# Inverse of the delta rule's unit triangular matrices: from full 128x128 tiles to compact 64x64 diagonal blocks

## The chip, the core and the metric

The kernel runs on one core of one Trainium2 chip. The metric is the device time of one execution in microseconds (us); the time before is the median of three executions. The engines are TensorE (PE in the profile, its weight loads PEld), VectorE (DVE), ScalarE (ACT), GpSimd (POOL) and SyncE (SP, which issues most transfers).

## What is computed

The program is one inference step of a two-layer encoder trunk, for a prompt of 512 rows and a second group of 32 rows. Its first mixer holds a gated delta rule with 4 heads, computed in chunks. For every chunk of L rows and every head the reference builds a unit lower triangular matrix and solves with it:

```python
gam = jnp.cumsum(g, axis=-1)
dec = jnp.exp(jnp.where(incl, gam[..., :, None] - gam[..., None, :], -jnp.inf))
kk = jnp.einsum('bhid,bhjd->bhij', k, k)
a_mat = jnp.eye(L) + jnp.where(strict, beta[..., :, None] * kk * dec, 0.0)
sol = lax.linalg.triangular_solve(a_mat, rhs, left_side=True, lower=True)
```

The kernel works on tiles of 128 rows. It inverts the matrix explicitly and keeps the transposed inverse in `a.xt`; the next phase multiplies with it. The rest of the program (projections, the other head group, attention, two mixtures of experts) is not touched.

## The kernel before

The program is a list of phases. Each phase is one or more blocks in which every engine has an instruction stream of its own; a barrier of all engines ends a block. The change lies in the second block of `phase_gdn_inverse`. Ahead of that block, the first block leaves the decayed products of the keys in `lm` (128 partitions, 5 tiles, 4 heads, 128 columns). Behind it comes `phase_gdn`, whose first work on the engines waits for the barrier.

The inverse is found by doubling. `LEV` is 7; at level l the blocks of 2^l rows on the diagonal are already inverted, and pairs of them are joined. A step is one level of one row tile t (all 4 heads together), and there are 7 x 5 = 35 steps, levels outside and tiles inside. One step i goes through four engines:

- POOL masks `lm` with the level's mask into `ll` (L1254, 128x512 elements).
- PE computes `ptt` from `ll` and `xt` (L1267, 4 matmuls of 128x128, one per head); the source calls this `product_t(i)`.
- ACT copies `ptt` to `tt` (L1294).
- PE computes `pp` (L1278, not at the last level) and `ppt` (L1279), 8 matmuls, called `correction(i)`; DVE subtracts them from `x` (L1303) and from `a.xt` (L1304).

PE's stream is product_t(i), then correction(i - 1). All buffers between the engines are double, and semaphores (`ll_ready`, `tt_done`, `tt_ready`, `p_done`, `x_ready`) count steps. The identity of level 0 is read from the constants `cst`.

One earlier phase, `phase_gla`, is quoted in the prediction because it already runs 64x64 matmuls (L1047, L1049, L1052). A 64x64 matmul uses one quarter of the array: the half of the input partitions is the row half, the half of the output partitions is the column half. Its output `gla_ps` is a PSUM tensor with 2 KB of each partition for each head, and `rows(h)` picks the row half by the head:

```python
for l in range(LEV - 1):
    for c, h in ((0, hs[0]), (1, hs[1]), (1, hs[0]), (0, hs[1])):
        m = em[rows(h), t % 2, l, at_col(c)]
        nc.tensor.matmul(ps[blk(c), h, l, :], m, m, start=True, stop=True)
...
for h in hs:
    last = nc.tensor.matmul(ps[0:HB, h, LEV, :], em[rows(h), t % 2, LEV - 1, at_col(0)],
```

Of the kernel before, what the change touches and what calls it, by code (L numbers as in the profile page):

```python
# [53 lines left out]
K_CS = K_ML + LEV * P  # L54
# [10 lines left out]
def constants():  # L65
# [7 lines left out]
    for l in range(LEV):  # L73
        m = 1 << l
        blk = i // m
        c[:, K_ML + l * P:K_ML + (l + 1) * P] = (blk[:, None] == blk[None, :] + 1) & (blk[None, :] % 2 == 0)
# [1111 lines left out]
def phase_gdn_inverse(g, a):  # L1188
# [5 lines left out]
    with ExitStack() as ctx:  # L1194
# [3 lines left out]
        x = sb("x", [P, NT, NH, P])  # L1198
        ll = sb("ll", [P, 2, NH, P])
        tt = sb("tt", [P, 2, NH, P])  # L1200
# [42 lines left out]
        ll_ready, tt_done, tt_ready, p_done, x_ready = map(sem, ("ll_ready", "tt_done", "tt_ready", "p_done", "x_ready"))  # L1243
        steps = LEV * NT
        ident = g.c(K_ID, P)
        with nc.Block() as block:
            @block.gpsimd
            def _(pool):
                for i in range(steps):
                    l, t = divmod(i, NT)  # L1250
                    if i >= 2:
                        pool.wait_ge(tt_done, i - 1)
                    mask = g.c(K_ML + l * P, P).unsqueeze(1).to_broadcast([P, NH, P])
                    nc.gpsimd.tensor_tensor(ll[:, i % 2], lm[:, t], mask, ALU.mult).then_inc(ll_ready, 1)  # L1254

            @block.tensor
            def _(pe):
                def product_t(i):

                    l, t = divmod(i, NT)  # L1260
                    pe.wait_ge(ll_ready, i + 1)
                    if l:
                        pe.wait_ge(x_ready, i - NT + 1)
                    if i >= 2:
                        pe.wait_ge(tt_ready, i - 1)
                    for h in range(NH):
                        last = nc.tensor.matmul(ptt[:, i % 2, h, :], ll[:, i % 2, h, :], a.xt[:, t, h, :] if l else ident, start=True, stop=True)  # L1267
                    last.then_inc(tt_done, 1)

                def correction(i):  # L1270

                    l, t = divmod(i, NT)
# [9 lines left out]
                for i in range(steps):  # L1282
                    product_t(i)
                    if i:
                        correction(i - 1)
                correction(steps - 1)

            @block.scalar
            def _(act):
                for i in range(steps):  # L1290
# [3 lines left out]
                    nc.scalar.copy(tt[:, i % 2], ptt[:, i % 2]).then_inc(tt_ready, 1)  # L1294

            @block.vector
            def _(dve):
                eye = ident.unsqueeze(1).to_broadcast([P, NH, P])
                for i in range(steps):
                    l, t = divmod(i, NT)  # L1300
                    dve.wait_ge(p_done, i + 1)
                    if l < LEV - 1:
                        nc.vector.tensor_tensor(x[:, t], x[:, t] if l else eye, pp[:, i % 2], ALU.subtract)  # L1303
                    nc.vector.tensor_tensor(a.xt[:, t], a.xt[:, t] if l else eye, ppt[:, i % 2], ALU.subtract).then_inc(x_ready, 1)  # L1304
# [1388 lines left out]
```

## Time and profile before

| | |
|---|---|
| median of three executions | 2523.39 us |
| lowest and highest | 2520.73 and 2523.8 us |
| the profiled execution | 2520.12 us |
| its span in the profile | 2518.2 us |
| mean granted TensorE clock | 0.907 of 2.4 GHz |
| PE busy over the span | 2066.4 us (82%) |
| DVE, ACT, POOL busy | 1600.8, 1301.5 and 261.8 us |

Times of the profile are counted from the start of the span. The span is 1.9 us shorter than the execution's own time, and the profiled execution lies 3.3 us below the median. Matmuls are recorded with modelled ends, so consecutive records overlap; the distance from start to start is the pace. An fp32 matmul leaves two records. The granted clock is 1.00 at 2.4 GHz and 0.50 at 1.2 GHz.

### The profile page before, as it was taken

The page shows a single profiled execution, that of the slowest core. Times are in us where ns is not written, and L with a number is a line of the kernel's source. Part 1 is how long each engine was busy: PE and PEld are TensorE (multiplying, and loading weights), DVE is VectorE, ACT ScalarE, POOL GpSimd, SP SyncE. Part 2 cuts the span into 40 slices and gives each one's busy share as a digit, 9 for nine tenths or more (in the row PEclk, how much of TensorE's full clock was granted, in tenths as well). Part 3 has the DMA queues.
Part 4 walks back from the last instruction along what each step waited for, and adds up shares of the span by engine and source line. Part 5 has one row for each costly group of instructions (what it writes and reads, how often), then busy time and mean ns, then how long its engine had stood idle before and what let it go on. Part 6 is the DMA issues. An engine that isn't in the chain of part 4 may idle for free. (4 is left out here: it accounts for less than half of the span.)

```text
span 2518.2 us, 32513 instructions
## 1 busy us (share of the span) xinstructions
PE 2066.4 (82%) x12936; PEld 1700.9 (68%) x12936; DVE 1600.8 (64%) x1729; ACT 1301.5 (52%) x1514; POOL 261.8 (10%) x329
## 2 busy tenths in 40 slices
PE   2689777886574999999998188998759999999990
PEld 1679774886574888888887054555747888888870
DVE  0345107454646888888886513665368888888883
ACT  1233612222323777777775342443237777777763
POOL 0123120330000010101110010000000010101000
PEclk6789888997786999999999598999969999999995
DMA  9167450000343899999997512002338999999974
GB/s 335 51 247 284 171 195 10 3 5 1 132 143 127 321 367 372 374 380 380 366 364 263 200 69 105 1 1 79 121 116 318 372 367 365 366 366 370 369 272 169
DMA packets 160041, 561.47 MB, mean 223 GB/s; under 512 B 33757, under 2 KB 39930, under 8 KB 126738
## 3 DMA queue, kind: packets, MB, share of 16 engines
q1 hardware_dynamic: 137938, 539.04, 57.9%
q0 software_dynamic: 21952, 20.32, 2.4%
q8 instruction: 106, 1.74, 0.3%
q14 instruction: 45, 0.37, 0.0%
HBM read 557.84 MB, written 50.70 MB: 242 GB/s over the span
## 5 line engine op out<-in xcount | busy, mean ns | idle before, releaser
L1954 DVE TENSOR_TENSOR ex_wl<-ring,ex_wh 128x2048 fp32r<-128x2048 f32 x384 | 867.9, 2289 | 112.5 <-ACT ex_wh L1909 112.5
L1909 ACT CAST ex_wh<-ring 128x2048 fp32r<-128x2048 f32 x384 | 712.4, 1910 | 0.0
L238 PE MATMUL ex_p<-ex_wh,ex_xh 128*128 128x512 f32 x1024 | 414.3, 405 | 8.3 <-DVE ex_xl L1959 8.3
L238 PE MATMUL ex_p<-ex_wl,ex_xh 128*128 128x512 f32 x1024 | 402.3, 393 | 0.0
L238 PE MATMUL ex_p<-ex_wh,ex_xl 128*128 128x512 f32 x1024 | 401.7, 392 | 0.0
L238 PEld LDWEIGHTS ex_p<-ex_wh,ex_xh 128*128 128x128 f32 x1024 | 194.5, 190 | 46.1 <-DVE ex_xl L1959 9.9
L238 PEld LDWEIGHTS ex_p<-ex_wl,ex_xh 128*128 128x128 f32 x1024 | 194.0, 189 | 42.7
L238 PEld LDWEIGHTS ex_p<-ex_wh,ex_xl 128*128 128x128 f32 x1024 | 194.5, 190 | 36.7
L238 PE MATMUL ex_py<-ex_wh,ex_gh 128*128 128x512 f32 x512 | 200.2, 391 | 2.8 <-DVE ex_gl L1975 2.8
L238 PE MATMUL ex_py<-ex_wl,ex_gh 128*128 128x512 f32 x512 | 200.2, 391 | 0.0
L238 PE MATMUL ex_py<-ex_wh,ex_gl 128*128 128x512 f32 x512 | 199.9, 390 | 0.0
L1823 POOL DMA_INDIRECT yrow<-ex_y,put x64 | 64.7, 1010 | 1026.9 <-ACT ex_y L1944 1026.9
L1922 ACT CAST ex_gh<-ex_pg 128x512 fp32r<-128x512 f32 x64 | 37.6, 588 | 155.1 <-PE ex_pg L1862 155.1
L1944 ACT COPY ex_y<-ex_py 128x1024 f32<-128x1024 f32 x64 | 65.1, 1017 | 92.4 <-PE ex_py L238 92.4
L238 PEld LDWEIGHTS ex_py<-ex_wh,ex_gh 128*128 128x128 f32 x512 | 96.6, 189 | 23.4 <-DVE ex_gl L1975 3.3
L238 PEld LDWEIGHTS ex_py<-ex_wh,ex_gl 128*128 128x128 f32 x512 | 96.6, 189 | 20.1
L238 PEld LDWEIGHTS ex_py<-ex_wl,ex_gh 128*128 128x128 f32 x512 | 96.5, 189 | 20.1
L1959 DVE TENSOR_TENSOR ex_xl<-ex_px,ex_xh 128x1024 fp32r<-128x1024 f32 x64 | 78.4, 1224 | 33.3 <-ACT ex_xh L1916 33.3
L270 DVE TENSOR_TENSOR ab_wl<-ring,ab_wh 128x2048 fp32r<-128x2048 f32 (+1 forms) x15 | 32.3, 2160 | 89.1 <-ACT ab_wh L265 89.1
L238 PE MATMUL ab_z<-ab_hh,ab_wh 128*128 128x288 f32 (+3 forms) x272 | 79.9, 294 | 4.4 <-DVE ab_wl L270 4.4
L1847 PEld LDWEIGHTS ex_px<-cst,ex_x 128*128 128x128 f32 x512 | 67.7, 190 | 22.2 <-DMA ex_x<-hrow,take 17.2
L1847 PE MATMUL ex_px<-cst,ex_x 128*128 128x128 f32 x512 | 68.7, 278 | 16.9 <-DMA ex_x<-hrow,take 16.9
(414 smaller groups left out, 3811.3 us busy)
## 6 DMA issues: line engine op xcount, KB each, us to landing
ring<-in_moe_w SPq DMA_DIRECT2D x384, 1024.0 KB, 7.3
ring<-in_ada_w SPq DMA_DIRECT2D x24, 2048.0 KB, 12.2
ring<-in_ab_w_in SPq DMA_DIRECT2D x7, 2048.0 KB, 9.7
mod<-mod SPq DMA_DIRECT2D x16, 512.0 KB, 7.1
cb_y<-yrow SPq DMA_DIRECT2D x16, 512.0 KB, 9.6
xres<-x SPq DMA_DIRECT2D x12, 512.0 KB, 2.7
x<-xres SPq DMA_DIRECT2D x12, 512.0 KB, 9.4
ring<-in_ab_w_out SPq DMA_DIRECT2D x2, 2048.0 KB, 11.9
```

What stands on the lines that cost most here:

```text
L238: ins = nc.tensor.matmul(out, a, b, start=first and n + m == 0, stop=last and n == len(terms) - 1 and m == 2)
L270: self.g.nc.vector.tensor_tensor(l, w, h.bitcast(F32), ALU.subtract).then_inc(self.lo_ready, 1)
L1823: pool.indirect_dma_start(out=io["yrow"], out_offset=bass.IndirectOffsetOnAxis(ap=rt.put[:, e:e + 1], axis=0), in_=y[:, e % 2, :], in_offs ...
L1847: last = nc.tensor.transpose(px[:, k, :], x[:, e % 2, k:D:KT], g.c(K_ID, P))
L1909: nc.scalar.copy(part(wh, u), g.view(base + u)).then_inc(hi_ready, 1)
L1922: nc.scalar.copy(gh[:], pg[:]).then_inc(gh_ready, 1)
L1944: nc.scalar.copy(y[:, (e - 1) % 2, :].rearrange("p (a n) -> p a n", a=2), py[:]).then_inc(y_ready, 1)
L1954: nc.vector.tensor_tensor(part(wl, u), g.view(base + u), part(wh, u).bitcast(F32), ALU.subtract).then_inc(lo_ready, 1)
L1959: nc.vector.tensor_tensor(xl[:, e % 2], px[:], xh[:, e % 2].bitcast(F32), ALU.subtract).then_inc(xl_ready, 1)
```

## The change

The 128x128 matrix of a tile is seen as two 64x64 diagonal blocks and one 64x64 block below them. The first six levels touch only the diagonal blocks. They are now held compactly: rows 0 to 63 of a tensor hold the upper block, rows 64 to 127 the lower one, both in 64 columns, so that every tensor of a step has 256 columns for the 4 heads. Each matmul of 128x128 becomes two of 64x64, one for each block, in different quarters of the array. Level 0 has no correction, since the blocks of one row are their own inverses: only `ptt` is computed, and DVE forms `x` and `xt` with four operations on 64 partitions. The last level computes only the block below the diagonal. For tile 4, which has 32 rows, levels 5 and 6 are dropped, which leaves 33 steps. POOL first sets the whole of `a.xt` to zero, and ACT first copies the diagonal blocks to `lmc`. The level masks in the constants shrink from 7 x 128 to 6 x 64 columns.

```diff
-K_CS = K_ML + LEV * P
+K_CS = K_ML + (LEV - 1) * HB
...
+        lmc = sb("lmc", [P, NT, NH, HB])
+        x, xt = sb("x", [P, NT, NH, HB]), sb("xt", [P, NT, NH, HB])
...
-        steps = LEV * NT
+        steps = [(l, t) for l in range(LEV) for t in range(NT) if t < NT - 1 or 1 << l < DSEQ]
+        place = {step: i for i, step in enumerate(steps)}
+        blocks = [slice(HB * c, HB * c + HB) for c in range(2)]
...
+                nc.gpsimd.memset(a.xt[:], 0.0).then_inc(zero_set, 1)
+                for i, (l, t) in enumerate(steps):
+                    if l == LEV - 1:
+                        break
+                    if l == 0:
+                        pool.wait_ge(lc_ready, t + 1)
                     if i >= 2:
                         pool.wait_ge(tt_done, i - 1)
+                        if steps[i - 2][0] == 0:
+                            pool.wait_ge(x_ready, i - 1)
+                    mask = g.c(K_ML + l * HB, HB).unsqueeze(1).to_broadcast([P, NH, HB])
+                    nc.gpsimd.tensor_tensor(ll[:, i % 2], lmc[:, t], mask, ALU.mult).then_inc(ll_ready, 1)
...
                     for h in range(NH):
-                        last = nc.tensor.matmul(ptt[:, i % 2, h, :], ll[:, i % 2, h, :], a.xt[:, t, h, :] if l else ident, start=True, stop=True)
+                        if l == LEV - 1:
+                            last = nc.tensor.matmul(ptt[blocks[0], i % 2, h, 0:HB], lm[blocks[1], t, h, 0:HB], a.xt[blocks[1], t, h, HB:P],
+                                                    start=True, stop=True)
+                            continue
+                        for r in blocks:
+                            last = nc.tensor.matmul(ptt[r, i % 2, h, 0:HB], ll[r, i % 2, h, :], xt[r, t, h, :] if l else g.cst[r, K_ID + r.start:K_ID + r.stop],
+                                                    start=True, stop=True)
                     last.then_inc(tt_done, 1)
...
                     for h in range(NH):
-                        if l < LEV - 1:
-                            nc.tensor.matmul(pp[:, i % 2, h, :], tt[:, i % 2, h, :], x[:, t, h, :] if l else ident, start=True, stop=True)
-                        last = nc.tensor.matmul(ppt[:, i % 2, h, :], x[:, t, h, :] if l else ident, tt[:, i % 2, h, :], start=True, stop=True)
...
+                        for r in blocks:
+                            nc.tensor.matmul(pp[r, i % 2, h, 0:HB], tt[r, i % 2, h, :], x[r, t, h, :], start=True, stop=True)
+                            last = nc.tensor.matmul(ppt[r, i % 2, h, 0:HB], x[r, t, h, :], tt[r, i % 2, h, :], start=True, stop=True)
...
+                for t in range(NT):
+                    nc.scalar.copy(lmc[blocks[0], t], lm[blocks[0], t, :, 0:HB])
+                    nc.scalar.copy(lmc[blocks[1], t], lm[blocks[1], t, :, HB:P]).then_inc(lc_ready, 1)
...
+                    if l == 0:
+                        dve.wait_ge(tt_done, i + 1)
+                        for r in blocks:
+                            nc.vector.tensor_tensor(x[r, t], eye(r), ll[r, i % 2], ALU.subtract)
+                            ins = nc.vector.tensor_tensor(xt[r, t], eye(r), ptt[r, i % 2, :, 0:HB], ALU.subtract)
+                        ins.then_inc(x_ready, 1)
+                        continue
                     dve.wait_ge(p_done, i + 1)
+                    if l == LEV - 1:
+                        nc.vector.tensor_scalar(a.xt[blocks[0], t, :, HB:P], ppt[blocks[0], i % 2, :, 0:HB], -1.0, None, ALU.mult).then_inc(x_ready, 1)
+                        continue
```

Two places of the instruction streams show the change. The first is POOL's stream at the start of the block, where `inv_ll` is the masked matrix; before, it begins with masks of 512 columns.

```order
L1254 ISA
L1254 TENSOR_TENSOR inv_ll<-inv_lm,cst 128x512 x2
L1254 TENSOR_TENSOR inv_ll<-inv_lm,cst 128x512 [waits inv_tt_done] x33
L1246 UNCONDITIONAL_BRANCH
```

Now POOL starts with the zeroing of `a.xt` (named gdn_xt), and its masks have 256 columns.

```order
L1255 MEMSET gdn_xt 128x2560
L1266 ISA
L1266 TENSOR_TENSOR inv_ll<-inv_lmc,cst 128x256 [waits inv_lc_ready] x2
L1266 TENSOR_TENSOR inv_ll<-inv_lmc,cst 128x256 [waits inv_x_ready,inv_tt_done,inv_lc_ready] x3
L1266 TENSOR_TENSOR inv_ll<-inv_lmc,cst 128x256 [waits inv_x_ready,inv_tt_done] x2
L1266 TENSOR_TENSOR inv_ll<-inv_lmc,cst 128x256 [waits inv_tt_done] x22
```

The masks of tiles 2 to 4 at level 0, and of the two steps behind them, now also wait for `x_ready`, since DVE itself reads `ll` at level 0. The second place is PE's stream at the start of the block. Before, eight matmuls of the first two products stand ahead of the first correction.

```order
L1267 MATMUL inv_ptt<-cst,inv_ll 128x128 x8
L1278 MATMUL inv_pp<-cst,inv_tt 128x128
L1279 MATMUL inv_ppt<-inv_tt,cst 128x128
L1278 MATMUL inv_pp<-cst,inv_tt 128x128
L1279 MATMUL inv_ppt<-inv_tt,cst 128x128
```

Now all five products of level 0 and the first two of level 1 stand there, in 56 matmuls of 64x64.

```order
L1285 MATMUL inv_ptt<-cst,inv_ll 64x64 x40
L1285 MATMUL inv_ptt<-inv_xt,inv_ll 64x64 x16
L1304 MATMUL inv_pp<-inv_x,inv_tt 64x64
L1305 MATMUL inv_ppt<-inv_tt,inv_x 64x64
L1304 MATMUL inv_pp<-inv_x,inv_tt 64x64
L1305 MATMUL inv_ppt<-inv_tt,inv_x 64x64
```

What moved: the first correction now belongs to step 5, and in each correction the two matmuls of the upper block stand ahead of the two of the lower block.

## Rows read from the trace of the kernel before

**Rows 1.** Windows of the block: length, busy of PE, PEld, DVE, ACT, POOL; clock, DMA share, GB/s.
```profile
463.20:467.40 4.20, 2.86 (x13) 2.87 (x14) 0.00 (x0) 0.59 (x1) 3.19 (x3) 0.59 0.01 2
467.40:556.30 88.90, 88.13 (x789) 87.94 (x787) 42.00 (x65) 19.89 (x34) 41.23 (x33) 1.00 0.01 1
```
**Rows 2.** Groups by line and shape from 330 to 600 us: busy, mean ns, idle before.
```profile
L1254 POOL TENSOR_TENSOR inv_ll<-inv_lm,cst 128x512 f32<-128x512 f32 x35 | 44.4, 1270 | 143.6 <-SPq L1246 99.8 <-PE inv_ptt L1267 43.8
L1279 PE MATMUL inv_ppt<-inv_tt,inv_x 128*128 128x128 f32 x240 | 43.8, 275 | 0.0
L1278 PE MATMUL inv_pp<-inv_x,inv_tt 128*128 128x128 f32 x200 | 38.7, 275 | 0.0
...
L1294 ACT COPY inv_tt<-inv_ptt 128x512 f32<-128x512 f32 x35 | 20.5, 585 | 72.2 <-PE inv_ptt L1267 72.2
L1304 DVE TENSOR_TENSOR gdn_xt<-gdn_xt,inv_ppt 128x512 f32<-128x512 f32 x30 | 20.4, 682 | 4.0 <-PE inv_ppt L1279 4.0
...
L1303 DVE TENSOR_TENSOR inv_x<-inv_x,inv_pp 128x512 f32<-128x512 f32 x25 | 17.2, 688 | 34.9 <-PE inv_ppt L1279 34.9
```
**Rows 3.** Timeline of the block: its start, one steady step, its end.
```profile
463.23 2.48 POOL L1254 TENSOR_TENSOR inv_ll<-inv_lm,cst 128x512 f32<-128x512 f32 x2 [99.80 <-SPq L1246]
...
464.54 3.40 PE L1267 MATMUL inv_ptt<-cst,inv_ll 128*128 128x128 f32 x16 [5.09 <-POOL inv_ll L1254]
...
472.24 1.06 PE L1267 MATMUL inv_ptt<-cst,inv_ll 128*128 128x128 f32 x8
...
474.92 1.06 PE L1267 MATMUL inv_ptt<-cst,inv_ll 128*128 128x128 f32 x8
...
555.57 0.69 DVE L1304 TENSOR_TENSOR gdn_xt<-gdn_xt,inv_ppt 128x512 f32<-128x512 f32 x1 [0.25 <-PE inv_ppt L1279]
```
**Rows 4.** Timeline of PE in the earlier phase with 64x64 tiles, clock 1.00.
```profile
404.71 0.93 PE L1047 MATMUL gla_ps<-gla_em 64*64 64x64 f32 x48 [1.88 <-DVE gla_qe L1142]
...
405.58 0.27 PE L1047 MATMUL gla_ps<-gla_em 64*64 64x64 f32 x2
405.60 0.28 PE L1052 MATMUL gla_ps<-gla_em 64*64 64x64 f32 x3
405.69 0.82 PE L1047 MATMUL gla_ps<-gla_em 64*64 64x64 f32 x44
...
406.51 0.30 PE L1052 MATMUL gla_ps<-gla_em 64*64 64x64 f32 x4
```
**Rows 5.** The same phase at the lower clock: timeline of PE, and its window.
```profile
435.06 1.56 PE L1047 MATMUL gla_ps<-gla_em 64*64 64x64 f32 x48 [4.84 <-DVE gla_qe L1142]
...
436.77 1.44 PE L1047 MATMUL gla_ps<-gla_em 64*64 64x64 f32 x44
...
433.40:440.10 6.70, 5.04 (x129) 4.60 (x130) 4.57 (x11) 0.19 (x1) 0.00 (x0) 0.50 0.08 22
```
**Rows 6.** Small operations elsewhere: a DVE pair in the timeline, then groups by shape.
```profile
403.81 0.85 DVE L1142 TENSOR_TENSOR gla_qe<-gla_em,gla_qk 64x256 f32<-64x256 f32 x2
...
L1148 DVE TENSOR_TENSOR gla_ket<-gla_ket,gla_ps 128x256 f32<-128x256 f32 x5 | 1.8, 416 | 2.9 <-ACT gla_ket L1105 2.9
L1117 ACT COPY gla_at<-gla_ps 64x256 f32<-64x256 f32 x5 | 1.8, 366 | 24.5 <-DVE gla_mk L1162 24.5
...
L1827 POOL MEMSET ex_x<- 128x2048 f32 x2 | 3.6, 1807 | 590.9 <-POOLq L1666 590.9
```
**Rows 7.** Two stretches with part of the array in use: window and PE's work.
```profile
139.70:143.10 3.40, 3.40 (x9) 2.18 (x9) 1.62 (x3) 1.91 (x3) 1.68 (x3) 0.50 0.11 37
...
139.22 4.76 PE L710 MATMUL ab_z<-w_alpha,lrT 25*128 25x256 f32 x10 [9.49 <-ACT lrT L747]
...
1491.40:1498.20 6.80, 6.80 (x26) 2.58 (x24) 1.59 (x8) 4.04 (x10) 0.00 (x0) 1.00 0.00 0
...
L2255 PE MATMUL mp_p<-ring,mla_hT 128*32 128x384 f32 x14 | 4.7, 486 | 0.0
```
**Rows 8.** The page, GB/s in 40 equal slices of the span.
```profile
GB/s 335 51 247 284 171 195 10 3 5 1 132 143 127 321 367 372 374 380 380 366 364 263 200 69 105 1 1 79 121 116 318 372 367 365 366 366 370 369 272 169
```

More of the change, by code:

```diff
@@ L75, in constants @@
         blk = i // m
-        c[:, K_ML + l * P:K_ML + (l + 1) * P] = (blk[:, None] == blk[None, :] + 1) & (blk[None, :] % 2 == 0)
+        if l < LEV - 1:
+            r, q = i[:, None] % HB >> l, i[None, 0:HB] >> l
+            c[:, K_ML + l * HB:K_ML + (l + 1) * HB] = (r == q + 1) & (q % 2 == 0)
         mid = blk // 2 * 2 * m + m - 1
@@ L1285, in _ @@
                         correction(i - 1)
-                correction(steps - 1)
+                correction(len(steps) - 1)
             @block.scalar
             def _(act):
-                for i in range(steps):
+                for t in range(NT):
+                    nc.scalar.copy(lmc[blocks[0], t], lm[blocks[0], t, :, 0:HB])
+                    nc.scalar.copy(lmc[blocks[1], t], lm[blocks[1], t, :, HB:P]).then_inc(lc_ready, 1)
+                for i, (l, t) in enumerate(steps):
+                    if l == 0:
+                        act.sem_inc(tt_ready, 1)
+                        continue
                     act.wait_ge(tt_done, i + 1)
@@ L1293, in _ @@
                         act.wait_ge(p_done, i - 1)
-                    nc.scalar.copy(tt[:, i % 2], ptt[:, i % 2]).then_inc(tt_ready, 1)
+                    r = blocks[0] if l == LEV - 1 else slice(0, P)
+                    nc.scalar.copy(tt[r, i % 2], ptt[r, i % 2, :, 0:HB]).then_inc(tt_ready, 1)
             @block.vector
             def _(dve):
-                eye = ident.unsqueeze(1).to_broadcast([P, NH, P])
-                for i in range(steps):
-                    l, t = divmod(i, NT)
-                    dve.wait_ge(p_done, i + 1)
-                    if l < LEV - 1:
-                        nc.vector.tensor_tensor(x[:, t], x[:, t] if l else eye, pp[:, i % 2], ALU.subtract)
-                    nc.vector.tensor_tensor(a.xt[:, t], a.xt[:, t] if l else eye, ppt[:, i % 2], ALU.subtract).then_inc(x_ready, 1)
+                ch = g.chain(dve, "dve")
@@ new lines, in _ @@
+                eye = lambda r: g.cst[r, K_ID + r.start:K_ID + r.stop].unsqueeze(1).to_broadcast([HB, NH, HB])
+                dve.wait_ge(zero_set, 1)
+                for i, (l, t) in enumerate(steps):
+                    if l == 0:
+                        dve.wait_ge(tt_done, i + 1)
[3 more added lines that the diff above has]
+                        ins.then_inc(x_ready, 1)
+                        continue
+                    dve.wait_ge(p_done, i + 1)
+                    if l == LEV - 1:
+                        nc.vector.tensor_scalar(a.xt[blocks[0], t, :, HB:P], ppt[blocks[0], i % 2, :, 0:HB], -1.0, None, ALU.mult).then_inc(x_ready, 1)
+                        continue
+                    if t < NT - 1 or 2 << l < DSEQ:
+                        nc.vector.tensor_tensor(x[:, t], x[:, t], pp[:, i % 2, :, 0:HB], ALU.subtract)
+                    if (l + 1, t) in place and l + 1 < LEV - 1:
+                        nc.vector.tensor_tensor(xt[:, t], xt[:, t], ppt[:, i % 2, :, 0:HB], ALU.subtract).then_inc(x_ready, 1)
+                    else:
+                        for r in blocks:
+                            ins = nc.vector.tensor_tensor(a.xt[r, t, :, r], xt[r, t], ppt[r, i % 2, :, 0:HB], ALU.subtract)
+                        ins.then_inc(x_ready, 1)
@@ L1307, in phase_gdn @@
+                g.done(ch, "dve")
 @phase
```

29 lines of the change are left out of this document (15 added, 14 removed).

## The prediction

> **What bounds the block now.** I read the windows first. From 467.40 to 556.30 us PE is busy 88.13 of 88.90 us at a granted clock of 1.00, while DVE has 42.00, POOL 41.23 and ACT 19.89 us of work, and the transfer engines stand at a share of 0.01 [rows 1]. So PE alone bounds the block, and no transfer waits in it. The groups say the same from the other side: PE's two correction groups have no idle time ahead of them, and ACT, DVE and POOL spend theirs waiting for PE [rows 2]. The timeline gives the price of a step: the products of two consecutive steps start at 472.24 and 474.92, 2.68 us apart, for 12 matmuls of 128x128, so 0.223 us each, two records of 0.112 [rows 3]. The block begins at 463.23 with POOL's first mask, and its last work is DVE's subtraction at 555.57, which ends at 556.26 [rows 3]. That is 93.03 us. The barriers at both ends stay, and the next phase starts from the barrier, so whatever the block gains the execution should gain: at 1 to 5 GB/s in the slices around it there is no stream of weights that would have to catch up [rows 8].
>
> **What a 64x64 matmul costs.** The block has none, the earlier phase has. With all four quarters of the array in use, 44 records start within 0.82 - 0.22 = 0.60 us, in 11 rounds of four, so one quarter takes a record each 0.06 us and a matmul of two records 0.12 us [rows 4]. (0.22 is the length of one record, which a last record adds.) The change uses two quarters at a time, upper left and lower right. The nearest row is L1052, two matmuls in two different row halves: its four records fit in 0.30 us [rows 4]. One after the other they would take 3 x 0.06 + 0.22 = 0.40; side by side 0.06 + 0.22 = 0.28. So two halves do run side by side, and a matmul costs 0.06 us in a dense stream of pairs. At 1.2 GHz the same reading gives (1.56 - 0.31) / 11 = 0.11 us for a record [rows 5], so 0.11 us a matmul in pairs and 0.22 alone. The bounds for a step of 24 matmuls at full clock are thus 24 x 0.06 = 1.44 us (pairs) and 24 x 0.12 = 2.88 us (each alone). I take 1.44, because L1052 is nearer.
>
> **Is anything else slower than 1.44 us?** DVE has two subtractions of 128x256, 0.42 us each [rows 6], 0.85 in all; at level 5 the second is split over two halves, and a pair of 64x256 takes 0.85 [rows 6], so 1.27. ACT has 0.37 to 0.38 for a copy of 256 columns, from the 64x256 row [rows 6]. POOL's mask of 512 columns takes 1.27 [rows 2]; half the columns cost between 0.64 and 1.27, and I take 0.68. All stay below 1.44, and the double buffers leave each a whole step, as now, so PE remains the bound through levels 1 to 5.
>
> **The new block, from 463.23.**
> - POOL sets 2560 columns to zero first: 1.81 us for 2048 [rows 6] gives 2.26. It hides nothing and nothing hides it: masks, products and DVE queue behind it. ACT's ten copies to `lmc` lie beside it; the first pair, 0.75 us, is done before the first mask, the rest keep ahead at 0.75 a tile. Uncovered they would cost that 0.75.
> - First mask 0.68, hand-overs 0.15 (in the block before, PE starts 0.07 after POOL's first mask ends [rows 3]), first product of 8 matmuls at the lower clock, 0.88 and 0.2 to finish: DVE starts level 0 at 467.4.
> - Level 0, five steps. DVE needs 4 x 0.425 = 1.70 us for each. But mask i + 2 waits until DVE has finished step i, since DVE reads `ll`, so two steps take 1.70 + 0.68 + 1.1 + 0.3 = 3.8 us, or 1.9 each; 9.5 in all, until 476.9. Step 6's mask waits for the last of them: PE's dense stretch starts at 477.7.
> - Levels 1 to 5, 24 steps (five tiles for levels 1 to 4, four for level 5): 24 x 1.44 = 34.6, less 0.5 for the product of step 5, which is done: until 511.8.
> - Clock. In the window 463.20:467.40 the clock is 0.59, after PE had stood idle, and from 467.40 it is 1.00, 2.9 us after PE's first matmul [rows 1, 3]; in the earlier phase PE works from 435.06 and the clock is still 0.50 up to 440.10 [rows 5]. Level 0 leaves PE idle half of the time, so I let the dense stretch begin at 1.2 GHz and run so for 5 us: 2.5 us lost, until 514.3.
> - Level 6, four steps of four products and four corrections in one quarter each: 0.48 + 0.48, and part of ACT's copy and its hand-overs no longer covered, 1.2 us a step: 4.8, until 519.1.
> - Last record and last DVE operation: 0.8, so 519.9.
>
> The gain is 556.26 - 519.9 = 36.4 us. The constants also shrink by 512 columns, 262 KB; at the first slice's 335 GB/s that is 0.8 us if that load is on the path [rows 8]. I count it as nothing, because the first weights stream beside it, and keep the 0.8 for the range. From the profiled execution's own 2520.12 us the sum gives 2483.7; the median lies 3.3 above that execution, so 2487.
>
> **Rivals.**
> 1. *The pairs overlap less, because of their order.* In a correction the two matmuls of the upper block stand ahead of the two of the lower one. If a matmul could start only after the one written before it, each pair of the same quarter would overlap the next pair in one record only: 2 x (0.24 - 0.06) = 0.36 us for four matmuls, a correction 1.44 and a step 1.92. That is 24 x 0.48 = 11.5 more: 2498.5. Against it: L1047's first two records of the next pair start at 405.58, before the L1052 records at 405.60 that are written ahead of them [rows 4], so a busy quarter doesn't hold up a free one. The Trainium skill (TensorE: Matmul & The Clock Gate, Part 3: Packing small matmuls) says that matmuls start and end in program order, which would bring this rival; the trace just quoted differs, and I go by the trace.
> 2. *The clock stays at 1.2 GHz.* Of the array's 16,384 cells two quarters use half. At 139.22 PE works densely for 4.76 us on 25 rows, and the clock stays 0.50 [rows 7]; against that, 26 records on 32 columns and all rows keep the clock at 1.00 over 6.8 us [rows 7]. The two quarters of a pair cover all rows, so the second row is the nearer one, but it shows only that a high clock stays. A step would cost 24 x 0.11 = 2.64, the levels 1 to 5 take 62.5 instead of 36.6, level 6 2.4 more: the gain shrinks to 8.1, 2515.
> 3. *The two blocks take turns, and it gets slower.* L1052's outputs lie in two separate stretches of 2 KB of PSUM, one for each head. Here the two blocks write the same stretch, `ptt[:, i % 2]`, on different partitions, from different row halves at the same time, and no row shows that. If the array made them take turns, a matmul would cost 0.12 and a step 2.88: 34.6 more, a gain of 1.8, 2521.6, no measurable change. But then only half of the rows would be at work at any time, and the clock would probably stay low as at 139.22: 0.22 a matmul, 5.28 a step, 54 us slower, 2578. It decides from 0.123 us a matmul, where 36.4 us are used up. The Trainium skill (TensorEngine Tiling (Array Packing), Gotcha 1: PSUM Pressure) says that different row tiles can't access one PSUM bank at the same time; no run here shows it yet. By it this rival would hold; without it the sum above.
>
> **Chances.** The forecast 0.60: both of its doubtful rows are near ones. Rival 1 0.12, rival 2 0.14, rival 3 0.12 (0.08 with the low clock, 0.04 without); 0.02 for anything else. The forecast's own range: if the clock rises before the dense stretch (2.5), level 0 runs at 1.70 (1.0), level 6 at 0.96 (1.0) and the constants count (0.8), it is 5.3 lower; with a mask of 0.9 us, a second slow stretch of the clock or level 6 at 1.7 it is about 6 higher: 2481 to 2493. For 8 in 10 the range has to take in rivals 1 and 2: 2480 to 2516, with some 0.14 outside. A measurement of this kernel can tell about 0.2%, 5 us, from no change: faster 0.87, same 0.05, slower 0.08.
>
> **What the profile after would show.** POOL's first instruction is a memset of 2.2 to 2.3 us. Products of consecutive steps in levels 1 to 4 start 1.44 us apart; 1.92 would be rival 1, 2.64 with a clock of 0.50 rival 2, 2.88 or 5.28 rival 3. DVE's groups of four 64x256 operations start 1.9 us apart. The granted clock reaches 1.00 within 5 us of the dense stretch. The block lasts about 57 us from POOL's first work to DVE's last, and the phases behind it are as long as before, but for a few us where the clock rises earlier or later in their gaps. The prediction is wrong if pairs that write one stretch of PSUM don't overlap, if half of the cells don't raise the clock, or if the time gained returns in a later phase.

## The result, and the profile after

| | before | after |
|---|---|---|
| median | 2522.06 us (4 runs) | 2485.39 us (4 runs) |
| lowest and highest | 2519.77 and 2523.8 us | 2483.24 and 2495.84 us |
| profiled execution, its span | 2520.12, 2518.2 us | 2486.33, 2484.5 us |
| block of the inverse, first work to DVE's last | 93.03 us | 55.45 us |

The changed kernel is 1.3% faster: the ratio is 0.9867, with a 95% interval from 0.9853 to 0.9881. The forecast was 2487.0 us, and a block of 56.7 us.

The windows of the new block come first (length, busy of PE, PEld, DVE, ACT, POOL, clock, DMA share, GB/s); they answer to [rows 1].

```profile
464.00:468.30 4.30, 1.21 (x22) 1.22 (x24) 0.00 (x0) 4.03 (x10) 3.63 (x3) 0.67 0.00 0
468.30:479.30 11.00, 5.24 (x80) 4.30 (x77) 8.80 (x20) 0.37 (x1) 3.94 (x6) 0.50 0.00 1
479.30:482.40 3.10, 3.10 (x57) 3.10 (x59) 0.18 (x1) 0.37 (x1) 1.35 (x2) 0.50 0.03 8
482.40:514.00 31.60, 31.16 (x1050) 30.89 (x1049) 17.11 (x46) 8.20 (x22) 14.54 (x20) 1.00 0.02 4
514.00:519.50 5.50, 4.53 (x107) 4.14 (x103) 4.15 (x11) 1.46 (x4) 0.00 (x0) 1.00 0.01 3
```

Read the second row first. In these 11 us of level 0, PE works 5.24 us, and DVE works 8.80: PE is no longer the bound there. In the third row PE is full, but at the clock of 0.50; only from 482.40 on is the block as it was before, PE full at 1.00.

The timeline of the same block (start, length, engine, line) answers to [rows 3].

```profile
464.04 2.23 POOL L1255 MEMSET gdn_xt<- 128x2560 f32 x1 [100.05 <-SPq L1252]
...
466.32 1.40 POOL L1266 TENSOR_TENSOR inv_ll<-inv_lmc,cst 128x256 f32<-128x256 f32 x2
...
467.09 1.97 PE L1285 MATMUL inv_ptt<-cst,inv_ll 64*64 64x64 f32 x32 [6.72 <-POOL inv_ll L1266]
...
468.33 0.42 DVE L1338 TENSOR_TENSOR inv_x<-cst,inv_ll 64x256 f32<-64x256 f32 x1 [4.58 <-PE inv_ptt L1285]
...
469.98 0.42 DVE L1338 TENSOR_TENSOR inv_x<-cst,inv_ll 64x256 f32<-64x256 f32 x1
...
474.21 0.42 DVE L1338 TENSOR_TENSOR inv_x<-cst,inv_ll 64x256 f32<-64x256 f32 x1
...
477.95 0.42 DVE L1339 TENSOR_TENSOR inv_xt<-cst,inv_ptt 64x256 f32<-64x256 f32 x1
...
479.30 1.12 PE L1285 MATMUL inv_ptt<-inv_xt,inv_ll 64*64 64x64 f32 x16 [1.33 <-POOL inv_ll L1266]
...
481.92 0.95 PE L1285 MATMUL inv_ptt<-inv_xt,inv_ll 64*64 64x64 f32 x16
...
483.61 0.68 PE L1285 MATMUL inv_ptt<-inv_xt,inv_ll 64*64 64x64 f32 x16
...
484.07 0.33 PE L1304 MATMUL inv_pp<-inv_x,inv_tt 64*64 64x64 f32 x4
...
484.19 0.33 PE L1305 MATMUL inv_ppt<-inv_tt,inv_x 64*64 64x64 f32 x4
...
485.01 0.68 PE L1285 MATMUL inv_ptt<-inv_xt,inv_ll 64*64 64x64 f32 x16
...
500.08 0.27 PE L1285 MATMUL inv_ptt<-inv_xt,inv_ll 64*64 64x64 f32 x2 [0.43 <-issue]
...
519.07 0.42 DVE L1344 TENSOR_SCALAR gdn_xt<-inv_ppt 64x256 f32<-64x256 f32 x1 [0.43 <-PE inv_ppt L1300]
```

The products at 483.61 and 485.01 are 1.40 us apart: this is a step at the full clock. At the low clock it is 481.92 - 479.30 = 2.62 us. The rows at 484.07 and 484.19 show more: the stream has `pp` and `ppt` of the upper block ahead of `pp` and `ppt` of the lower one, yet the four records of the two `pp` start first and the four of the two `ppt` after them. So the lower `pp` starts ahead of the upper `ppt`, which is written before it.

The 37.6 us that the block gained lie as follows, each stretch read from the starts of its products in both traces:

| stretch | before | after |
|---|---|---|
| first work to the first product of level 1 | 463.23 to 477.60, 14.4 us | 464.04 to 476.86, 12.8 us |
| to the first product of level 6 | to 544.60, 67.0 us for 25 steps | to 513.94, 37.1 us for 24 steps |
| to DVE's last | to 556.26, 11.7 us for 5 steps | to 519.49, 5.6 us for 4 steps |

Some 27 of the 37.6 us come from the shorter steps of levels 1 to 5, and 2.7 from the step that is dropped there; level 6 gives 6.1, of which its dropped step was 1.8. Level 0 gives 1.6 only, although it lost all of its corrections.

Two of the groups by line answer to [rows 2]:

```profile
L1304 PE MATMUL inv_pp<-inv_x,inv_tt 64*64 64x64 f32 x384 | 26.1, 223 | 0.0
...
L1266 POOL TENSOR_TENSOR inv_ll<-inv_lmc,cst 128x256 f32<-128x256 f32 x29 | 21.2, 734 | 23.8 <-PE inv_ptt L1285 16.1 <-DVE inv_xt L1339 7.6
```

The corrections still run without idle time ahead of them. In POOL's row the last part is new: 7.6 us in which a mask (mean 734 ns) waits for DVE at level 0.

### The profile page after: what moved, and what is told of

Same layout as the page of the kernel before. It is cut to its first block and busy times, and to the rows that moved or that the text cites. A ratio compares the mean times of both kernels' runs of the same rounds, so it can differ in the third digit from the quotient of the medians.

```text
span 2484.5 us, 33518 instructions
## 1 busy us (share of the span) xinstructions
PE 2023.5 (81%) x13432; PEld 1655.3 (67%) x13432; DVE 1588.6 (64%) x1740; ACT 1295.6 (52%) x1517; POOL 240.8 (10%) x324
## 5 line engine op out<-in xcount | busy, mean ns | idle before, releaser
L1972 ACT CAST ex_gh<-ex_pg 128x512 fp32r<-128x512 f32 x64 | 37.6, 588 | 154.5 <-PE ex_pg L1912 154.5
```

The source lines that it names most:

```text
L1972: nc.scalar.copy(gh[:], pg[:]).then_inc(gh_ready, 1)
```

## Experiments

The questions are two. The theory of the prediction: in levels 1 to 5 two quarters of the array run side by side, and this is what makes the gain; its rivals were the order, the clock and turns. And second: what do the 18 us up to 482.4 cost, and what paces them? "Block" is always from the block's first work to DVE's last, in one profiled execution; the changed kernel's own was 55.5 us long in the first and 54.1 in the second one (f1), so a difference of 1.5 us in that length alone is not told from chance. The runs e1 to e8 are one execution each, and the changed kernel's own eight lie between 2483.24 and 2495.84 us: of their whole times only e3's and e4's stand out, and the others are read from the block. The expectations of f2 and f3 count a block 0.2 to 0.3 us longer (55.7, 51.3 and 48.2 us for 55.5, 51.1 and 47.9). A comparison with "the changed kernel" below is with its median of 2485.39 us.

**e4: half of the matmuls.** This kernel leaves out the work of PE, ACT and DVE on the lower 64x64 blocks in levels 1 to 5.

```diff
-                        for r in blocks:
+                        for r in blocks[0:1] if l else blocks:
...
-                        for r in blocks:
+                        for r in blocks[0:1]:
                             nc.tensor.matmul(pp[r, i % 2, h, 0:HB], tt[r, i % 2, h, :], x[r, t, h, :], start=True, stop=True)
...
```

> Levels 1 to 5 leave out the lower block: its matmuls, its part of ACT's copy and of DVE's subtractions. The output of the lower rows is therefore only level 0's. PE works in one quarter of the array at a time, which is what rival 3 of the prediction (the blocks take turns) would have looked like. Theory of rival 3: half of the rows do not bring the clock up, it stays at 1.2 GHz through the levels, and a step of 12 matmuls takes 12 x 0.22 = 2.6 us. Opposite theory: dense work in one quarter is enough, the clock rises within 5 us as in the changed kernel, and a step takes 12 x 0.117 = 1.40 us.

It took 2512.0 us, 26.6 more than the changed kernel with twice the matmuls; the block is 81.1 us long. Its window over the levels 1 to 5 and two products of consecutive steps:

```profile
480.00:539.00 59.00, 59.00 (x558) 59.00 (x559) 16.91 (x46) 8.42 (x23) 15.80 (x22) 0.50 0.01 2
```
```profile
500.52 1.06 PE L1285 MATMUL inv_ptt<-inv_xt,inv_ll 64*64 64x64 f32 x8
...
503.08 1.06 PE L1285 MATMUL inv_ptt<-inv_xt,inv_ll 64*64 64x64 f32 x8
```

A step of 12 matmuls takes 2.56 us, 0.213 each, at a clock of 0.50, although PE is busy for all of the 59 us. So with one quarter in use a full PE does not raise the clock here, and with two it does. The low clock of rival 3's second branch is thus a real danger; the change escapes it only because its pairs run together.

**e3: the same matmuls, upper half first.** A correction issues eight matmuls of the upper block and then eight of the lower one.

```diff
-                    for h in range(NH):
...
                         for r in blocks:
-                            nc.tensor.matmul(pp[r, i % 2, h, 0:HB], tt[r, i % 2, h, :], x[r, t, h, :], start=True, stop=True)
+                            for h in range(NH):
+                                nc.tensor.matmul(pp[r, i % 2, h, 0:HB], tt[r, i % 2, h, :], x[r, t, h, :], start=True, stop=True)
...
```

> In a correction all eight matmuls of the upper block stand ahead of the eight of the lower block. If PE could look past any number of matmuls that wait for a busy quarter, steps would stay 1.40 us. If it looks only a few matmuls ahead, as I expect, the first of the eight lower ones starts late: with a look-ahead of 2 matmuls the upper eight take 8 x 0.117 = 0.94 us with 2 of the lower beside them, and the lower run on with the next product beside them, so a step grows to about 1.40 + 0.5 = 1.9 us, and the block by 24 x 0.5 = 12 us to 67. Without any overlap between the two groups a step would be 0.47 + 1.87 = 2.34.

It took 2546.22 us, 60.8 more than the changed kernel, and 20.8 more than the execution of the kernel before that was measured beside it (2525.41). The block is 105.3 us long. The rows are a piece of one correction (the two x4 rows are where the upper half ends and the lower one begins), two products of consecutive steps, and the window.

```profile
480.61 0.42 PE L1305 MATMUL inv_pp<-inv_x,inv_tt 64*64 64x64 f32 x2
480.82 0.42 PE L1306 MATMUL inv_ppt<-inv_tt,inv_x 64*64 64x64 f32 x2
481.03 0.48 PE L1305 MATMUL inv_pp<-inv_x,inv_tt 64*64 64x64 f32 x4
481.25 0.48 PE L1306 MATMUL inv_ppt<-inv_tt,inv_x 64*64 64x64 f32 x4
481.52 0.42 PE L1305 MATMUL inv_pp<-inv_x,inv_tt 64*64 64x64 f32 x2
...
500.42 0.78 PE L1285 MATMUL inv_ptt<-inv_xt,inv_ll 64*64 64x64 f32 x10
...
503.95 0.79 PE L1285 MATMUL inv_ptt<-inv_xt,inv_ll 64*64 64x64 f32 x10
```
```profile
479.00:563.20 84.20, 84.20 (x1140) 84.20 (x1141) 18.62 (x49) 8.93 (x24) 15.65 (x22) 0.50 0.01 2
```

From 480.61 to 481.03 there is one matmul each 0.21 us; from 481.03 to 481.52 four matmuls take 0.49. A free quarter does run ahead of a busy one, but only by a few matmuls: where the two halves meet, four of the sixteen find a partner, and a few more at the two ends, beside the products. A step takes 3.53 us, against 2.62 with all in pairs at the same clock. That is 24 x 0.91 = 22 us for the order. The rest of the block's 50 us is the clock: it is 0.50 from 464.5 us to the end of the block, 24 x (2.62 - 1.40) = 29, less the 1.5 that the changed kernel also loses. My expectation counted the order alone and was wrong by 38 us. Of the 60.8 us, 8 lie in a later phase (see f2).

**e2: pairs next to each other.** Upper `pp`, lower `pp`, upper `ppt`, lower `ppt`: the upper block's two matmuls no longer stand ahead of the lower one's two.

```diff
                             nc.tensor.matmul(pp[r, i % 2, h, 0:HB], tt[r, i % 2, h, :], x[r, t, h, :], start=True, stop=True)
+                        for r in blocks:
                             last = nc.tensor.matmul(ppt[r, i % 2, h, 0:HB], x[r, t, h, :], tt[r, i % 2, h, :], start=True, stop=True)
```

> In a correction the upper and lower block's matmuls alternate (upper, lower, upper, lower) where the changed kernel has two upper and then two lower. Theory (a busy quarter does not hold up a free one): steps stay 1.40 us apart. Rival (order costs something that the pipeline only partly hides): steps get shorter than 1.40, down to the 24 x 2 x 0.053 / 2 = 1.28 us that the two passes of 64 columns would take at 2.4 GHz without gaps.

It took 2485.06 us, and the steps are the same, 1.40 us:

```profile
484.36 0.63 PE L1285 MATMUL inv_ptt<-inv_xt,inv_ll 64*64 64x64 f32 x16
...
485.76 0.63 PE L1285 MATMUL inv_ptt<-inv_xt,inv_ll 64*64 64x64 f32 x16
```

So the order that the change has costs nothing against this one: with two matmuls of a quarter in a row the other quarter still reaches its partner, with eight it does not.

**e1: zeroing in the block before.** POOL has no other work there.

```diff
+                @block.gpsimd
+                def _(pool):
+                    nc.gpsimd.memset(a.xt[:], 0.0).then_inc(zero_set, 1)
...
-                nc.gpsimd.memset(a.xt[:], 0.0).then_inc(zero_set, 1)
```

> The zeroing of a.xt moves to POOL's stream of the first block, where POOL has no work. Theory: the memset is uncovered in the changed kernel (2.23 us ahead of the first mask, 464.04 to 466.32 in its trace), so the block shrinks from 55.4 us to about 54.0: the first mask now waits for the first pair of copies to lmc, 0.85 us, so 1.4 us come off, not 2.2. Rival: the zeroing only delays a level that waits for DVE anyway, and the block stays at 55.4.

It took 2482.26 us. The new start of the block:

```profile
462.40 0.41 ACT L1321 COPY inv_lmc<-inv_lm 64x256 f32<-64x256 f32 x1 [1.45 <-PEq L1210]
...
463.30 1.56 POOL L1270 TENSOR_TENSOR inv_ll<-inv_lmc,cst 128x256 f32<-128x256 f32 x2 [15.85 <-ACT inv_lmc L1322]
...
464.08 1.97 PE L1289 MATMUL inv_ptt<-cst,inv_ll 64*64 64x64 f32 x32 [5.36 <-POOL inv_ll L1270]
```

The first product starts 1.68 us after the block's first work instead of 3.05. So 1.4 of the memset's 2.23 us are won; ACT's first two copies, 0.8 us, which it had covered, are now on the path. The dense stretch starts 13.9 us after the block's first work, for 15.3 in the changed kernel's two executions, and the block is 53.9 us long, as expected. Its length alone shows little: it is 54.1 us in f1 and 54.3 in e2, which keep the memset. In e1 the second and a later step of the dense stretch took 2.09 and 1.93 us, where f1 has 1.51 and 1.40, and this takes back most of the earlier start.

**e5: PE kept busy with unread products.**

```diff
+                idle_work(7)
                 for i in range(len(steps)):
                     product_t(i)
+                    if steps[i][0] == 0:
+                        idle_work(3)
```

> TensorE gets extra 128x128 products of the identity into a PSUM tensor that nobody reads: seven at the start of the block, three behind each product of level 0. In the changed kernel the dense stretch starts at 479.30 us and runs 3.1 us at a granted clock of 0.50. If the low clock comes from TensorE's idle time at level 0, the clock reads 1.00 when the dense stretch starts, steps are 1.40 us from its first on, and the block is 1.4 to 2 us shorter than the changed kernel's 55.7 us: about 2484 us in all. Rival: three extra products at 0.44 us each make a step of level 0 cost TensorE 0.88 + 1.32 = 2.2 us at the lower clock, over VectorE's 1.7, and level 0 becomes 1 to 2 us longer, which takes the gain back: 2485 to 2487.

It took 2481.03 us; the block is 53.5 us long. The clock is 0.99 in the second window, where the changed kernel still had 0.50:

```profile
463.50:471.50 8.00, 7.06 (x58) 6.33 (x58) 2.71 (x7) 4.03 (x10) 4.36 (x4) 0.58 0.00 0
471.50:479.50 8.00, 6.02 (x100) 4.99 (x100) 5.93 (x14) 0.37 (x1) 3.77 (x5) 0.99 0.01 4
```

So more of PE's work at level 0, here of full 128x128 products, lifts the clock there. In the six profiles with this level 0 and no extra products (the changed kernel, f1 and e1 to e4) it is still 0.50 when the dense stretch begins. That PE's idle time alone keeps it low does not follow, and e8 speaks against it. From 480.47 on the steps take 1.40 us, which saves most of the 1.5 us that the clock costs; level 0 itself is not shorter.

**e6: level 0 with corrections.** The shortcut is undone: ACT's copy and PE's correction are back, and DVE reads `pp` and `ppt`. With it goes the masks' wait for DVE.

```diff
-                        if steps[i - 2][0] == 0:
-                            pool.wait_ge(x_ready, i - 1)
...
-                    if l == 0:
-                        pe.sem_inc(p_done, 1)
-                        return
...
-                            nc.vector.tensor_tensor(x[r, t], eye(r), ll[r, i % 2], ALU.subtract)
+                            nc.vector.tensor_tensor(x[r, t], eye(r), pp[r, i % 2, :, 0:HB], ALU.subtract)
...
```

> Level 0 is done as the other levels, with ScalarE's copy and TensorE's correction, so the shortcut of the change is undone and the masks wait for nothing of VectorE's. Theory A: the shortcut brings nothing here, because VectorE needs four operations of 0.43 us a step either way (1.7 us), and TensorE, now dense from the first product on, gets the higher clock some 4 us after it. Level 0 then ends no later than now (about 477.5 us against 479.3), level 1 starts at the high clock, and the block is 2 to 3 us shorter: 52.5 to 54 us, 2482 to 2484 us in all. Theory B: the shortcut pays; the corrections at the lower clock cost 2.6 us a step for all of level 0, 13 us against 11, and the block is 58 us long: 2488.

One execution took 2488.18 us, but the block is only 51.1 us long, 3.0 to 4.4 shorter than in the two profiles of the changed kernel. Theory A holds for the block. **f2** is the same kernel in five executions, measured beside **f1**, the changed kernel again, in four.

> Level 0 with corrections, as in e6, whose block was 51.3 us long against 55.7, while its one execution was no shorter than the changed kernel: 8 us appeared in a normalisation phase at 1772 us that has nothing to do with the block. If the block is what counts and those 8 us belong to that one execution, the median is 4 us under that of the changed kernel of the same call, about 0.2% (between 3 and 5). Rival: the 8 us come back in most executions, because the later phases now start at other times, and the median is equal to or above the changed kernel's.

> The changed kernel itself, beside the kernel before and the two below. Its ratio to the kernel before should be 0.985 to 0.988, as in the first result.

f1: median 2486.73 us (2485.81 to 2488.31), ratio to the kernel before 0.987, interval 0.9855 to 0.9885. f2: 2478.58 us (2477.4 to 2483.23), ratio 0.9842, interval 0.9829 to 0.9856. That is 8.2 us under the changed kernel measured beside it, twice what I had expected; f1 came out as expected. The windows of level 0 in f2, and the start of its products:

```profile
465.30:470.20 4.90, 4.81 (x91) 4.81 (x93) 0.94 (x3) 2.12 (x6) 2.25 (x5) 0.51 0.00 0
470.20:478.30 8.10, 8.10 (x265) 8.01 (x263) 7.35 (x20) 2.06 (x6) 4.30 (x6) 1.00 0.03 6
```
```profile
470.83 0.68 PE L1283 MATMUL inv_ptt<-cst,inv_ll 64*64 64x64 f32 x16
...
472.23 0.68 PE L1283 MATMUL inv_ptt<-cst,inv_ll 64*64 64x64 f32 x16
...
473.70 0.68 PE L1283 MATMUL inv_ptt<-inv_xt,inv_ll 64*64 64x64 f32 x16
...
475.26 0.68 PE L1283 MATMUL inv_ptt<-inv_xt,inv_ll 64*64 64x64 f32 x16
```

PE is busy from the first product on (465.39), and the clock is up at 470.2, 4.8 us after it; in the changed kernel it was up 15.3 us after it (467.09 to 482.4). Once the clock is up, a step of level 0 costs 1.40 to 1.56 us with its correction, less than the 2.1 us without. f2's block is 52.6 us long, 1.5 shorter than f1's. The 8 us of e6's execution did not come back in f2's profile. They lie in one normalisation phase; its windows in e6 and then in f2:

```profile
1772.60:1807.20 34.60, 22.91 (x120) 22.15 (x120) 15.33 (x16) 16.19 (x23) 0.00 (x0) 0.51 0.44 146
```
```profile
1773.10:1799.60 26.50, 14.78 (x120) 14.10 (x120) 15.32 (x16) 16.19 (x23) 0.00 (x0) 0.71 0.54 190
```

The same 120 matmul records take 22.91 us at a clock of 0.51 and 14.78 at 0.71. In e3's execution this phase is 34.6 us long at 0.50 too. It says nothing of the block.

Nor does the block explain f2's 8.2 us. The two profiled executions lie 7.5 us apart: 1.5 in the block, 2.0 in the phase behind it, 1.0 in a projection ahead of it, and 2.5 in the phase of transfers near the end (10.4 us in f1, 7.9 in f2), in which PE has no work; the rest is in small differences. The last one takes 7.8 to 8.0 us in some kernels and 9.7 to 10.4 in others, and about the same again in each kernel that was profiled twice (10.1 and 10.4 with the shortcut, 8.0 and 7.9 without, 10.0 and 9.9 in e7 and f3 below). What sets it is open.

**e7: level 0 without brakes.** The zeroing as in e1; the masks of level 0 have a buffer for each tile (`l0`) and don't wait for DVE; DVE does two operations on 128 partitions with a compact identity (`ec`) in place of four on 64.

```diff
...
-                        for r in blocks:
-                            nc.vector.tensor_tensor(x[r, t], eye(r), ll[r, i % 2], ALU.subtract)
-                            ins = nc.vector.tensor_tensor(xt[r, t], eye(r), ptt[r, i % 2, :, 0:HB], ALU.subtract)
-                        ins.then_inc(x_ready, 1)
+                        nc.vector.tensor_tensor(x[:, t], eye, l0[:, t], ALU.subtract)
+                        nc.vector.tensor_tensor(xt[:, t], eye, ptt[:, i % 2, :, 0:HB], ALU.subtract).then_inc(x_ready, 1)
```

> Level 0 without its three brakes: the zeroing of a.xt lies in the block before, the masks of level 0 have a buffer for each tile and wait for nobody, and VectorE does two operations of 128x256 a step on a compact identity instead of four of 64x256. If my reading of level 0 holds, a step costs about 1 us (product 0.88 at the lower clock, two VectorE operations 0.85) in place of 2.1, DVE starts 1.4 us earlier, and the dense stretch starts 7 us earlier than in the changed kernel, counted from the block's start. Block 48 to 49.5 us, about 2479 us in all. Rival: the clock rises as many microseconds later as the dense stretch starts earlier, since the same time at work is needed; then 1 to 2 us of it are lost: block 50 to 51, 2480.

It took 2480.61 us with a block of 47.9 us. The first DVE operation of step 1 and of step 3:

```profile
465.82 0.61 DVE L1343 TENSOR_TENSOR inv_x<-inv_ec,inv_l 128x256 f32<-128x256 f32 x1
...
468.24 0.61 DVE L1343 TENSOR_TENSOR inv_x<-inv_ec,inv_l 128x256 f32<-128x256 f32 x1
```

Two steps take 2.42 us, 1.21 each, for the 4.23 / 2 = 2.1 of the changed kernel (469.98 to 474.21 above). **f3** is the same kernel in five executions, measured beside f1 and f2.

> The level 0 without brakes, as in e7, whose block was 48.2 us long against 55.7 and starts 0.7 to 1.6 us earlier, since the zeroing is not in it. Median 7 to 8.5 us under that of the changed kernel of the same call, a ratio of about 0.983 to the kernel before. Rival: part of it is lost where the experts' weights stream (601.3 us for the first of those phases in e7's execution against 598.0), and only 4 to 5 us remain.

Its block was 46.6 us long, but its five executions spread from 2477.24 to 2490.28, with a median of 2484.28 and a ratio of 0.9858 (0.9841 to 0.9876). The median is 2.4 us under f1's, less than either expectation (7 to 8.5, and 4 to 5 for the rival), and the expected ratio of 0.983 lies outside the interval. The rival named the right phase: in both profiled executions the first phase of experts lasts 601.3 us against 597.8 to 598.2 in the others, as it did before the change (601.3); this takes back 3.3 of the 7.5 us that the block gained. In the first 60 us of that phase f3 has 197 records of PE and 252 GB/s of transfers, f1 has 208 and 262, both at a clock of 0.84. So it is not the clock; what it is, is not settled.

**e8: both.** e7 with extra products, four at the start and one behind each product of level 0.

```diff
+                idle_work(4)
...
+                    if steps[i][0] == 0:
+                        idle_work(1)
```

> The level 0 of e7 with extra 128x128 products of the identity into an unread PSUM tensor: four at the block's start, one behind each product of level 0. If they lift the clock before the dense stretch, the block is 1.4 us shorter than that of e7: about 47 us, 2477.5 us in all. Rival: each extra product costs TensorE 0.44 us at the lower clock, which makes TensorE the bound of level 0 at 1.3 us a step, and the block is as long as that of e7 or up to 1 us longer.

It took 2477.92 us, yet the block is 52.1 us long, 4.2 more than e7's. PE's products of level 0, and a window:

```profile
468.39 1.12 PE L1290 MATMUL inv_ptt<-cst,inv_l 64*64 64x64 f32 x16
469.44 0.79 PE L1315 MATMUL inv_pd<-cst 128*128 128x128 f32 x2
470.17 1.12 PE L1290 MATMUL inv_ptt<-cst,inv_l 64*64 64x64 f32 x16
...
475.49 1.97 PE L1290 MATMUL inv_ptt<-inv_xt,inv_ll 64*64 64x64 f32 x32
...
478.95 0.93 PE L1290 MATMUL inv_ptt<-inv_xt,inv_ll 64*64 64x64 f32 x16
```
```profile
469.00:479.00 10.00, 10.00 (x131) 8.63 (x130) 3.25 (x8) 0.87 (x3) 3.84 (x6) 0.50 0.01 2
```

A step costs 1.77 us, since one extra product takes 0.73 us where I had counted 0.44, and the clock rose only at 479.6. The extra work was paid, and the clock did not come, although PE is busy for all 10 us of the window. So a busy PE is not enough by itself. In e5, with three 128x128 products behind each product of level 0, the clock rose 5.1 us after the first product (466.57); here, with one, it took 12.9 (from 466.62). How much of that is the kernel is open: between e7 and f3, one kernel, it varies too, 9.2 us (463.65 to 472.8) against 3.7 (464.45 to 468.2). That the execution is short all the same lies elsewhere: its second phase of experts takes 598.8 us, for 601.5 to 603.0 in the others.

**g1: corrections, early zeroing, wide operations.** f2 with e1's zeroing and e7's two DVE operations; ACT makes `ec` between its copies.

> Level 0 with corrections, as in f2, and in addition the zeroing of a.xt in the block before, and two VectorE operations of 128x256 a step of level 0 on a compact identity instead of four of 64x256. The first product should start 1.7 us after the block's first work instead of 3.05, and a step of level 0 should take 1.40 us instead of 1.55 once the clock is up: a block of about 50 us, and a ratio to the kernel before of 0.983 to 0.984, 1 to 3 us under f2's 2478.6 us. Rival: the block is shorter, but what the later phases vary by from execution to execution (as in f3, 2477 to 2490) hides it, and the ratio stands anywhere from 0.983 to 0.987.

Median 2481.87 us (2480.46 to 2491.08), ratio 0.9844 (0.9828 to 0.9861), which can't be told from f2's. The profiled block is 52.0 us long, not 50. PE and ACT show why:

```profile
469.15 0.48 PE L1305 MATMUL inv_pp<-cst,inv_tt 64*64 64x64 f32 x4 [1.00 <-ACT inv_tt L1328]
```
```profile
464.01 0.40 ACT L1321 COPY inv_lmc<-inv_lm 64x256 f32<-64x256 f32 x1 [1.45 <-PEq L1211]
...
468.73 0.65 ACT L1328 COPY inv_tt<-inv_ptt 128x256 f32<-128x256 f32 x2
```

PE's first product is earlier, but its correction waits 1.00 us for ACT, which has to finish the twelve copies of the start first. The memset had covered them. The clock is at 0.50 until about 472.3, 6.6 us after the first product (465.69), for 4.8 in f2.

## Why the prediction came out right

The block of 55.45 us, by the prediction's steps, whose times are shifted by the 0.8 us by which the block starts later (464.04 against 463.23):

- **Start to DVE's first work**: 4.29 us, forecast 4.2. The memset was 2.23 (forecast 2.26), a mask 0.70 to 0.86 (0.68).
- **Level 0 to the dense stretch**: 468.33 to 479.30, 10.97 us; forecast 10.3. The loop of waits was the one named: two steps take 4.23 us, not 3.8.
- **Steps of levels 1 to 5**: 1.40 us each, forecast 1.44. The 0.06 us that I had read for a record was 0.058. The bounds of the step, 1.44 and 2.88, were decided at the lower end. What the upper one rests on is seen in e4, at the lower clock: one quarter alone takes 2.56 us for half of the matmuls, where pairs take 2.62 for all.
- **Clock**: it rose 3.1 us after the dense stretch began, and two steps took 2.62 and 1.69 us: 1.5 us lost, forecast 2.5. One gap of 0.6 us between starts at 499.4, which no wait explains (the row at 500.08 has 0.43 of it as "issue"), was not foreseen. From 479.30 to the last correction of level 5, at 515.3: 36.0 us, forecast 36.6.
- **Level 6 and the end**: 515.3 to 519.49, 4.2 us, forecast 5.6. The products of level 6 need another quarter of the array than the corrections, and their records start among those of corrections: the first starts at 513.94, the last record of the correction written ahead of it at 514.11.

The sum is 1.25 us under the forecast. The block gained 37.6 us, the span 33.7 (2518.2 to 2484.5). The other 3.9 us are spread over phases that the change doesn't touch: the block starts 0.8 later, the phase behind it is 0.8 longer, the projection of the second mixer 0.9, a combination 1.5, a phase of transfers near the end 2.0, the first experts are 3.1 shorter, and about 1 us lies in small differences. e6 and f2, one kernel, differ by 8 us in one phase, so part of this is chance. But the phase of transfers and the first experts repeat: f1, the changed kernel again, has them at 10.4 and 597.9 us, where the first profile has 10.1 and 598.1. So the claim that the execution gains what the block gains held to about 4 us, a tenth of the gain, and why these phases moved is open.

The closeness of the median is in part luck. The prediction's sum for the profiled execution was 2483.7 us, and that execution took 2486.33, 2.6 over: the block came out 1.25 better, and the other phases took 3.9 back. The 3.3 us that were then added, because the profiled execution before lay so far below its median, don't hold for the changed kernel, whose profiled execution lies 0.9 above its median. The two misses cancel but for 1.6 us.

One term was put at nothing, the shorter constants (0.8 us). The first phase, which loads them, is 46.4 us long, for 47.2 before, and 46.2 to 46.8 in the twelve other profiles with the short constants. There is one profile with the long ones, so this only suggests that the 0.8 us were won; the phases between it and the block are longer by more than that.

**Rival 1** (order) is refuted for the order that the change has by the step of 1.40 us, where it wanted 1.92, and by e2; e3 shows the mechanism in a milder form than the rival's: a free quarter runs ahead, but not by eight matmuls. The Trainium skill (TensorE: Matmul & The Clock Gate, Part 3: Packing small matmuls) has matmuls start and end in program order; in the changed kernel's trace the lower `pp` starts ahead of the upper `ppt` (484.07 and 484.19), and in e3's a few matmuls pass others, so the measurement differs from the Trainium skill in the small.

**Rival 2** (two quarters don't raise the clock) is refuted by the fourth window of the block. It was a near thing: with one quarter (e4) or with pairs half broken (e3) it came true. The prediction's reason, that the two quarters of a pair cover all rows, is not enough: e8's pairs and full products cover all rows too, and PE was busy at 0.50 for over 12 us. That the clock rose within the 5 us allowed for it was in part luck.

**Rival 3** (turns on one PSUM stretch) is refuted: the 16 records of a product start within 0.46 us (483.61 to 484.07), although both blocks write `ptt[:, i % 2]`. The Trainium skill (TensorEngine Tiling (Array Packing), Gotcha 1: PSUM Pressure) says that different row tiles can't access one PSUM bank at the same time; with 64x64 tiles in different row and column halves, on different partitions, this trace shows no turns.

One step of the prediction was never asked: whether the shortcut at level 0 is worth anything. I costed it and did not weigh it against the level as it was. As it is built here, it isn't: without it the block is 51.1, 52.6 and 52.0 us long (e6, f2, g1), with it 55.5, 54.1 and 54.3 (the changed kernel, f1, e2), and f2's median is 8.2 us lower than f1's. Of these 8.2 the block explains 1.5 only, and the rest is open. It is not the shortcut in itself that costs: with its waits removed the block is shorter still, 47.9 and 46.6 us (e7, f3), though there too the clock is 0.50 when level 0 starts. But f3's executions did not get shorter by as much.

By its median the best version that was run several times is f2: all levels alike, in pairs of 64x64. Its interval (0.9829 to 0.9856) overlaps with those of g1 and f3, so it is not shown to be better than they are.

## What to carry to other kernels

Small matmuls in separate quarters of the array paid here when the stream alternated the quarters every one or two matmuls; with eight of one quarter in a row the same work was slower than the full 128x128 matmuls it replaced, more by the low clock (28 us) than by the lost pairs (22). Groups between two and eight were not tried. When a change takes work away from the engine that sets the pace, look at what that leaves idle: here the saved corrections of level 0 left PE half empty, and the low clock and a loop of waits took back more than they had cost. Without that loop (e7, f3) the shortcut did shorten the block. And a block that is 7.5 us shorter made the median 2.4 us shorter: measure the whole as well. What covers what changes with the cover, too: taking the memset off the path put ACT's copies on it.

## Of the hardware, not expected

- A PE that is busy for 59 us with 64x64 matmuls in one quarter stays at a granted clock of 0.50 (e4), and one with half broken pairs for 84 us as well (e3). With pairs it rose 3.1 us after the dense stretch began.
- PE busy for 10.00 of 10.00 us with 64x64 pairs and single 128x128 products between them stayed at 0.50 too (e8).
- One kernel in two executions (e7, f3): the clock rose 9.2 and 3.7 us after the first product of level 0.
- A free quarter passes a busy one by a few matmuls, not by eight (e3).
- The same normalisation phase took 26.5 or 34.6 us in executions of one kernel, by the clock alone (0.71 or 0.51).
